# Second retrieval level on 112 sums and a 16-bit decode, with the one-hot batches in two long operations spread over 84 steps of the first expert pass

## What is computed

```python
s = jnp.einsum('nhpd,hpkd->nhpk', q, sub_keys)        # 8 heads, 2 halves, 128 keys
s1, i1 = lax.top_k(s[:, :, 0], 16)
s2, i2 = lax.top_k(s[:, :, 1], 16)
cand = (s1[..., :, None] + s2[..., None, :]).reshape(n, 8, 256)
cidx = (i1[..., :, None] * 128 + i2[..., None, :]).reshape(n, 8, 256)
top, pos = lax.top_k(cand, 16)
eidx = jnp.take_along_axis(cidx, pos, axis=-1)
gates = jax.nn.softmax(top, axis=-1)
...
act = gelu(einsum('nd,nhed->nhe', x, expert_u[eidx]))
y = einsum('nhe,nhed->nd', gates * act, expert_v[eidx])
```

## Time and profile before

| | us |
|---|---|
| median of three executions | 1992.9 |
| the profiled execution | 1994.66 |
| its span, first to last instruction | 1992.9 |
| PE busy | 1835.5 (92%) |
| DVE busy | 1564.3 (78%) |
| POOL busy | 931.9 (47%) |
| ACT busy | 650.6 (33%) |
| mean granted TensorE clock, share of full | 0.952 |
| U pass, first U matmul to first V matmul | 686.3 to 1391.2 |
| V pass, first matmul to the last one's start | 1391.2 to 1970.7 |

### The profile page before, as it was taken

One profiled execution on the slowest core, in us unless ns is written; L12 is line 12 of the kernel. 1 busy time (PEld: TensorE's weight loads), 2 busy tenths in 40 slices (PEclk: granted clock), 3 DMA queues, 4 the chain that ended last, 5 costly groups with the idle time before them and its releaser, 6 DMA issues.

```text
span 1992.9 us, 29861 instructions
## 1 busy us (share of the span) xinstructions
PE 1835.5 (92%) x11654; PEld 1774.0 (89%) x11654; DVE 1564.3 (78%) x2754; ACT 650.6 (33%) x1037; POOL 931.9 (47%) x676
## 2 busy tenths in 40 slices
PE   5999567887989999999889999997999999999998
PEld 4999566765989999899889999997999999999997
DVE  4797777755459989999899999944788888888852
ACT  4443211112133332222333434432333333333332
POOL 2899897000000258788756566665133334333200
PEclk9999698865989999999999999998999999999999
DMA  7221100001552258787569999999899999999841
GB/s 203 70 77 51 37 1 0 1 1 39 151 170 75 71 173 286 249 275 268 199 205 303 305 304 297 302 333 384 293 364 395 346 364 351 354 344 363 316 172 35
DMA packets 192957, 424.87 MB, mean 213 GB/s; under 512 B 11236, under 2 KB 119296, under 8 KB 184617
## 3 DMA queue, kind: packets, MB, share of 16 engines
q1 hardware_dynamic: 155505, 287.99, 41.9%
q0 software_dynamic: 37312, 134.97, 19.5%
HBM read 361.28 MB, written 62.06 MB: 212 GB/s over the span
## 4 chain that ended last, share of the span: by engine, by line
PE 64%; DVE 26%; issue 3%; DMA 2%; POOL 2%; ACT 2%; SPq 0%; DVEq 0%; ACTq 0%
PE psum L1157 29%; PE psum L1137 14%; PE psum L827 7%; PE psum L1125 4%; PE psum L822 3%; PE psum L915 2%; DMA rowg<-in_expert_u_rows,idx 2%; DVE sel L1938 1%; DVE eqa L1935 1%; DVE junk L1960 1%; DVE cT L1611 1%; DVE besti L1887 1%; DVE WR L1540 1%; DVE sring L1891 1%; PE psum L973 1%
## 5 line engine op out<-in xcount | busy, mean ns | idle before, releaser
L1137 PE MATMUL psum<-xT,WS 128*128 128x416 f32 x3072 | 607.4, 357 | 21.8 <-POOL WS L764 21.4
L1137 PEld LDWEIGHTS psum<-xT,WS 128*128 128x128 f32 x3072 | 580.1, 191 | 30.7 <-POOL WS L764 25.1
L1157 PE MATMUL psum<-AR,WS 128*128 128x416 f32 x3072 | 579.8, 351 | 2.6 <-DVE AR L2048 2.6
L1157 PEld LDWEIGHTS psum<-AR,WS 128*128 128x128 f32 x3072 | 575.0, 188 | 7.5 <-DVE AR L2048 3.0
L764 POOL TENSOR_TENSOR WS<-RAWP,WS 128x1024 fp32r<-128x1024 f32 x128 | 311.7, 2437 | 496.9 <-ACT WS L1438 495.9
L757 POOL DMA_INDIRECT rowg<-in_expert_v,idx x128 | 177.5, 1386 | 315.2 <-DVE acc L1973 305.6
L827 PE MATMUL psum<-xT,WR 128*128 128x280 f32 (+1 forms) x1968 | 261.3, 296 | 2.7 <-DVE xT L1566 2.7
L827 PEld LDWEIGHTS psum<-xT,WR 128*128 128x128 f32 x1968 | 258.4, 193 | 3.4 <-DVE xT L1566 3.2
L1448 ACT ACTIVATE WS<-RAWP 128x1024 fp32r<-128x1024 f32 x128 | 135.8, 1061 | 348.1 <-PE psum L1157 335.5
L2041 DVE TENSOR_TENSOR WS<-RAWP,WS 128x1024 fp32r<-128x1024 f32 x128 | 156.6, 1224 | 117.6 <-ACT WS L1448 117.6
L1475 ACT ACTIVATE actA<-psum 128x416 f32<-128x416 f32 x128 | 66.3, 518 | 447.8 <-PE psum L1137 411.9
(11 more groups left out here) (326 smaller groups left out, 1937.9 us busy)
## 6 DMA issues: line engine op xcount, KB each, us to landing
RAWP<-in_expert_u SPq DMA_DIRECT2D x64, 1024.0 KB
RAWP<-in_expert_v SPq DMA_DIRECT2D x64, 1024.0 KB
act_dram<-actA SPq DMA_DIRECT2D x128, 208.0 KB
gate_dram<-gblk SPq DMA_DIRECT2D x13, 2048.0 KB, 11.9
Gt<-gate_dram SPq DMA_DIRECT2D x32, 832.0 KB
act<-act_dram SPq DMA_DIRECT2D x64, 416.0 KB
RAW<-in_w_in SPq DMA_DIRECT2D x8, 1024.0 KB, 5.4
RAW<-in_w_query SPq DMA_DIRECT2D x8, 1024.0 KB, 5.6
```

The source lines that it names most:

```text
L1137: last = mm(bank[e % 2][:, 0:TD], ws(e)[:, pw, kt * P:(kt + 1) * P], xT[:, px, kt, TSP:TPE], start=(kt == 0 and i == 0), stop=(kt == KT - ...
L1157: last = mm(bank[dt][:, 0:TD], ws(NK + e)[:, pw, dt * P:(dt + 1) * P], AR[:, e % 4, pa, :], start=(e == 0 and i == 0), stop=(e == NK - 1 a ...
```

## The change: what it does

- **Level two on 112 sums.** With both lists sorted, sum (a, b) can be among the 16 largest only if (a + 1)(b + 1) <= 16. The kernel now forms all 16 sums for a < 4 and the first 4 for a >= 4: 64 + 48 = 112 per head in place of 256.
- **16-bit decode.** The index of the first list is found as a telescoped sum: `topb >= firsts` (4096 16-bit elements, both lists in one operation) times the steps between successive indices `stepb`, and four halving additions in place of the two reductions.
- **Tiles weighed singly.** The exponential, the division by the sum and PE's transposes go tile by tile: `EXP_AT` has five entries (17, 25, 31, 49, 67), `WEIGH_AT` and `PAIRS_AT` tie DVE's parts to batch numbers. All transposes use bank 7, and the batches use three PSUM banks in place of four.
- **One-hot batches of two operations**: one compare on 2048 and one product on 3072 16-bit elements, in place of two and three on 1024.
- **Batches over steps 33 to 116**: batch b stands behind step 33 + 83b // 51, so that 1 or 2 steps lie between batches. Level two of tiles 3 and 4 is run inside the batches, one stage per batch in the first 18 (a tile has 9 stages now).
- **Dots spread**: 14 dot products before the first batch, up to number 17 with the first, then 100 over all 52 batches, so 1 or 2 in each, and 12 after the last. The gathers follow: from step 19 (before 12), the last eight one per step from step 119 (before three per step).
- `actA` has four buffers (before two), gate blocks are of 16 tokens (before 32), a load of gates covers 8 steps of the V pass (before 4), `junk` has one buffer, gathered rows are accumulated from V step 5 (before 8), the final norm's weights are loaded in the V pass.

Core of the diff:

```diff
+WIDE, NARROW = 4, 4
+NCAND = WIDE * TOPK + (TOPK - WIDE) * NARROW
-GB = 32
+GB = 16
+GE = 8
-EXP_S_AT, EXP_D_AT = 10, 57
-PAIR_AT = {58 + i: 1 + i for i in range(ND)}
-GATE_AT = {62 + b: b for b in range(NBAT)}
-G2_AT = 121
-L2DOTS = 48
+GATE0, GATE_END = 33, 116
+def gate_at(b):
+    return GATE0 + (GATE_END - GATE0) * b // (NBAT - 1)
+GATE_AT = {gate_at(b): b for b in range(NBAT)}
+PAIR_AT = {GATE0 - 4: 1, gate_at(5): 2, gate_at(17): 3, gate_at(28): 4}
+EXP_AT = {17: 0, GATE0 - 8: 1, GATE0 - 2: 2, gate_at(10): 3, gate_at(21): 4}
+WEIGH_AT = {2: 2, 14: 3, 25: 4}
+PAIRS_AT = {8: 2, 20: 3, 32: 4}
+G2_AT = GATE_END + 7
+DOTS_PRE, DOTS_IN = 16, 100
+def dots_by(b):
+    return DOTS_PRE + DOTS_IN * (b + 1) // NBAT
 GATHER_AT = {}
 for _s in range(PAIRS):
-    if _s < L2DOTS + 4:
-        _n = 12 + 9 * _s // 10
...
+    if _s < DOTS_PRE + 4:
+        _n = 19 + max(_s - 3, 0)
+    elif _s < DOTS_PRE + DOTS_IN + 4:
+        _n = gate_at(min(b for b in range(NBAT) if dots_by(b) > _s - 4)) + 2
     else:
-        _n = 119 + (_s - (L2DOTS + 8 + NBAT)) // 3
+        _n = GATE_END + 3 + (_s - DOTS_PRE - DOTS_IN - 4)
     GATHER_AT.setdefault(_n, []).append(_s)
...
+                op(sums(0, WIDE, TOPK))
+                at_ = WIDE * TOPK
+                chain(sums(WIDE, TOPK, NARROW))
...
+                chain(tt(ev.rearrange("p (h x) a r -> p h x a r", x=2),
+                         topb[0:n].rearrange("p (h x) r -> p h x r", x=2).unsqueeze(3).to_broadcast(all_),
+                         firsts[0:n].unsqueeze(1).to_broadcast(all_), ALU.is_ge))
+                yield
+                e2 = ev.rearrange("p c a (r j) -> p c a r j", j=2)
+                chain(tt(e2, e2, sb.unsqueeze(3).to_broadcast([n, 2 * PH, TOPK, TOPK // 2, 2]), ALU.mult))
+                yield
+                for m, a_, b_ in ((8, ev, lv), (4, lv, ev), (2, ev, lv)):
+                    a2 = a_[:, :, 0:2 * m, :].rearrange("p c (a two) r -> p c a two r", two=2)
+                    chain(tt(b_[:, :, 0:m, :], a2[:, :, :, 0, :], a2[:, :, :, 1, :], ALU.add))
...
+                chain(tt(by_two(oh[:, i]), keys_, per_token(0, 2), ALU.is_equal))
+                by_three = [P, 3, OHB * NK // 2, 2]
+                second = oh[:, i, 1].rearrange("p t (k j) -> p (t k) j", j=2).unsqueeze(1).to_broadcast(by_three)
+                tt(by_two(ohg[:, i]), second, per_token(2, 5), ALU.mult).then_inc(oh_ready, 1)
...
+            for i, _ in enumerate(level_two(1)):
+                if i in (4, 6, 8):
                     next_dot()
-                if t == 1:
-                    A.wait(dve, "gexp", 0)
-                    weigh(0, 1, P)
...
+            for i, _ in enumerate(level_two(2)):
                 next_dot()
+                if i == 5:
+                    weigh(0)
+                    weigh(1)
+            next_dot()
+            next_dot()
+            pair_values(1)
+            later = (None for t in range(3, NTP) for _ in level_two(t))
             for b in range(NBAT):
...
+                if b in WEIGH_AT:
+                    weigh(WEIGH_AT[b])
+                if b in PAIRS_AT:
+                    pair_values(PAIRS_AT[b])
+                one_hots(b)
+                while issued[0] < dots_by(b):
+                    next_dot()
+                next(later, None)
```

More of the change, by code:

```diff
@@ L58 @@
 DB = TD // ND
+WIDE, NARROW = 4, 4
+NCAND = WIDE * TOPK + (TOPK - WIDE) * NARROW
+assert all((a + 1) * (NARROW + 1) > TOPK for a in range(WIDE, TOPK))
 NTP = 1 + ND
@@ L1953, in _, with pair_values, by_batch, twice @@
-            dots = iter(range(PAIRS))
+                chain(tt(gv, gv, gs.unsqueeze(2).to_broadcast([n, PH, TOPK]), ALU.mult), "gates", t)
+            def pair_values(t):
+                T.wait(dve, "pairT", t)
+                b_ = bank[7]
+                g_ = b_[:, 2 * DB:3 * DB]
+                nb_ = DB // OHB
+                pv = pairs[:, (t - 1) * nb_:t * nb_]
+                def by_batch(v):
+                    return v.rearrange("p (b i) -> p b i", i=OHB)
+                def twice(v):
+                    return by_batch(v).unsqueeze(3).to_broadcast([P, nb_, OHB, 2])
+                for x in range(2):
+                    op(dve.tensor_copy(pv[:, :, x], twice(b_[:, x * DB:(x + 1) * DB])))
+                chain(dve.tensor_copy(pv[:, :, 2], twice(g_)))
+                chain(tt(by_batch(gtmp[:, 0]), by_batch(g_), pv[:, :, 2, :, 0], ALU.subtract), "pairT", t)
+                chain(dve.tensor_copy(pv[:, :, 3], twice(gtmp[:, 0])))
+                chain(tt(by_batch(gtmp[:, 1]), by_batch(gtmp[:, 0]), pv[:, :, 3, :, 0], ALU.subtract))
+                chain(dve.tensor_copy(pv[:, :, 4], twice(gtmp[:, 1])))
@@ L1963, in next_dot @@
             def next_dot():
-                for s_ in dots:
-                    dot(s_)
-                    return
+                dot(issued[0])
+                issued[0] += 1
             def axpy(s_):
```

228 lines of the change are left out of this document (110 added, 118 removed).

## The result

The changed kernel takes **2001.1 us** (median of 8 runs, 1997.1 to 2005.4); the kernel before, run beside it, 1991.5 (8 runs, 1984.3 to 1996.9). The ratio is 1.0052, 95% interval 1.0031 to 1.0073: half a per cent slower, where the forecast was 1978, 0.7% faster. The size lies inside the range of the forecast, the sign does not.

What follows compares the result with a forecast made beforehand. PE bounds the kernel, but DVE, slowed by collisions with POOL's subtraction, paces the first eighteen batches: 1994.7 - 47.9 + 32 = 1978.8, given as 1978 us after the 1.8 to the median; range 1950 to 2006.

Steps and rivals of the forecast that it cites:

- The floor and the prize: U pass: 4.54 us per step plus 1.41 per batch gives floor 654.4 against 704.9; 47.9 us can be won.
- no delay: Batch 18: at 0.6 us lost per subtraction DVE is ready at 998.4, so the kernel takes 1947 us.
- The first batch: Start of the batches: DVE ready at 840, PE through step 33 at 840.7; DVE has no lead.
- DVE's clean work: First eighteen batches: one-hots, dots, two tiles, weighings and pair values take DVE 141 us without collisions.
- rival 3: One-hot batches: product on 3072 elements runs at fp32 rate, 3.4 us instead of 1.75; 2038 us; slower outcomes together 0.14.
- the price of a collision in the first eighteen batches: DVE against POOL there: 29 subtractions at 1.68 us, 48.7 us, so batch 18 ready at 1029.7.
- rival 2: First eighteen batches: collisions are complete, 29 x 2.09 = 61 us, kernel 1991, up to 2003; chance 0.21.
- The row behind 1.68: Settled batches of the kernel before: compare 2356 against 679 ns, medians and minimum of 52, gives 1.68 us per subtraction.
- Behind batch 18: Later batches: DVE needs 8.0 us per batch, with 1.68 per subtraction, against PE's 8.8; PE bounds again.
- PE's waits: First eighteen batches: PE waits for DVE some 30 us in total, beat from batch to batch about 10.5 us.
- Its upper end: Price of one POOL subtraction to DVE: at most 2.09 us, the whole loss of the case at 725.69.
- The end of the pass: U pass from step 117 on: no stop over 1 us; the 2.6 us handover stays; V pass from about 1375.

Runs made afterwards that it cites:

- experiment 1: Changed kernel with POOL's subtraction cut to 16 of 1024 columns for steps 36 to 64; 1955.9 us, ratio 0.9819 to the kernel before.
- experiment 6: Changed kernel's new operations put back in the order of the kernel before (batches over steps 62 to 113, level two ahead); 1966.2 us, ratio 0.9881.
- experiment 4: Changed kernel with gathers issued four steps behind their batch's step instead of two; 1971.8 us, ratio 0.9898 to the kernel before.
- 3: Changed kernel with level two of tiles 3 and 4 in every second batch, over 36 batches; 1962.1 us, ratio 0.9845 to the kernel before.
- experiment 7: Changed kernel with a batch's one-hots made in five operations on 1024 elements again; 2028.4 us, ratio 1.0189 to the kernel before.
- experiments 8 to 10: Changed kernel, level two in every second batch from the third, no dot product in batch 0; 9 and 10: gathers four, three steps behind; 1959.5, 1965.9, 1961.0 us.

## Why the forecast was wrong

**The floor and the prize: the beat was right, the floor was not reached.** Behind batch 18 and to the V pass everything runs at the beat that the forecast read. The best versions stay 12 us above the 1947 that it gave for no delay, and even experiment 1 stays 9 above it. (The forecast took the 1.8 us to the median off its 1978.8, but not off 1947 and 1990.7.)

**The first batch: 5 us off.** Forecast 840 from DVE and 840.7 from PE; it came at 845.6. Both were late: PE was through step 33 at 845.0, after four stops for POOL (2.5 us), and then waited 0.61 us for DVE's product, which ended at 845.57. The forecast called such stops hidden behind DVE; they were, but only because DVE itself was 5.6 us later than its sum. Which term of that sum was short was not followed. DVE had indeed no lead.

**DVE's clean work: right.** 2048 and 3072 elements take 1.226 and 1.758 us (forecast 1.21 and 1.75), which puts out rival 3. The 205.0 us of the stretch less 59.8 of collisions and 4.8 idle are 140.4, forecast 141.

**The step that failed is the price of a collision in the first eighteen batches**: "29 subtractions", "so I take 1.68: 48.7 us". It measured 2.0 each over 30, 59.8 us. With the late start (5.6), 11.1 more of collisions, and DVE's 4.8 of idle gaps that the sum did not have, less the 0.6 of clean work, batch 18 comes at 1050.6 instead of 1029.7. The V pass then begins 23 us later than forecast and the total is 23 us above it. In the changed kernel that is rival 2 in price and nearly in its order of events ("the second, asked for meanwhile, goes in front"; here both go in front of one operation). Its own time, 1991, lacks the start and the gaps. The other 2 us of the 23 lie behind batch 18, where the pass takes 347.7 us for 345.6.

The row behind 1.68 was right for what it shows: in the settled batches of before 43 subtractions in 250 us came one at a time, and the eight single ones here cost 1.68 each as well. Wrong was to take all 29 as single. The forecast itself said that POOL would stand at gathers until a batch's dots are done; it did not draw what follows, that with one or two steps between two batches a POOL that stands through them has two subtractions due when it is let go, and that a pair is paid in full. Eleven pairs cost 46.4 - 22 x 1.68 = 9.4 us more than single ones, and the thirtieth subtraction 1.7: the 11.1.

The larger part was not priced by anyone: even 1.68 is not one price for all places. It belongs to a POOL that comes again and again at the same point of DVE's round, just when a two-input operation begins. In the kernel before and in experiment 6 the beat of the steps keeps it there, with ACT's cast letting POOL go (1.68 and 1.87); in the changed kernel DVE's own dot products do. In experiment 4, where the places change, the same instructions cost 0.9 each, and in 3, where DVE has slack, 1.0. That the place explains all of the fall is argued; the runs show the price and the rows that go with it, not each cause by itself.

**Behind batch 18: the right result, the size too high.** The compare and the product there have means of 1.494 and 2.704 us, so with two small operations some 46 us over 55 subtractions, 0.84 each, not 1.68. Here DVE is ahead and waits for PE to free its buffers (47.2 us, 24 times), and collisions cost half as much. In experiment 7 DVE does not get ahead, and they cost 2.4 each up to 1320 us; its batches also hold 0.3 us more of clean work, so the run does not tell which of the two keeps DVE late.

**PE's waits: right, and misleading.** "Some 30 us in total" were forecast and 32.6 measured, while the beat from batch to batch was 11.4 us and not "about 10.5". Beside them stand 16 us more in which PE works at a lower granted clock. As long as DVE paces, these are no cost of their own, but the sum of PE's waits is then no measure of the loss either: that is 48 us.

**The Trainium skill's rule.** The forecast set beside rival 2 what the Trainium skill says (SBUF — State Buffer, "Who interferes with whom"): the pair of ports is an exclusive lock, and issue order decides who blocks. Its upper end was 2.09 per subtraction, and a subtraction of a pair costs 2.1: so far the trace agrees. The order, read by the starts in the trace, does not come out so: DVE's product started at 862.50 while the first subtraction ran, the second started at the end of the first, and still the second went first. That DVE's operation is held to the end of the run of subtractions is so in all eleven pairs, and for runs of three and four in experiments 8 to 10. DVE does not keep the ports in the same way. In the kernel before its two compares follow each other without a gap, and a subtraction that starts during the first goes in front of the second:

```profile
1014.35 0.69 DVE L2023 TENSOR_TENSOR oh<-iotab,pairs 128x1024 bf16<-128x1024 bf16 x1
1014.44 2.87 POOL L764 TENSOR_TENSOR WS<-RAWP,WS 128x1024 fp32r<-128x1024 f32 x1 [9.48 <-ACT WS L1438]
...
1014.95 2.91 DVE L2024 TENSOR_TENSOR oh<-iotab,pairs 128x1024 bf16<-128x1024 bf16 x1
```

Why the one engine keeps them and the other does not, no run shows.

**The end of the pass: right.** One stop of PE behind step 117 remains, the 2.6 us of the handover, and the V pass is 579.5 us long to its last matmul's start, as before.

## What to carry to other kernels

When two engines share a port, count not only how often they meet but how the other engine's work is released: an engine that was held at a wait does its saved-up work in one burst, and whoever asks meanwhile pays for the whole burst, be it two, three or four operations. Before work of the critical engine is moved between the pieces that another engine waits for, see that it enters with a lead, or spread it so that a lead forms; here every second batch instead of every batch was worth 39 us with the same operations. And before a contention price is taken from a row, see where in the critical engine's round the other one arrives, and whether alone: here the same subtraction cost 1.7 to 1.9 us alone at a fixed place, 2.1 in a pair, and 0.9 where its place changed.

## What was not expected of the hardware

- A short DVE operation caught between two back-to-back GpSimd subtractions waits for both: 4.10 us for 0.29 us of work, 5.09 for 0.68, up to 5.62 for the compare of 1.22. Such a pair itself takes 4.73 to 4.77, twice the 2.4 of one: it loses nothing. Runs of three and four hold 0.27 us of work for 7.68 and 10.00.
- Who pays shifts with the place: 2407 ns per subtraction in the changed kernel, 2788 in experiment 4, where more of them start during an operation of DVE, with DVE's loss falling from 60 to 27 us.
- The 16-bit operations with a repeated operand (3072 elements, one input repeated three times) keep the full rate: 1.758 us against 1.226 for 2048, 0.53 per 1024 elements.
